# A layer stack on one core: the adaptive-norm weight pieces go to GpSimd's DMA queue, the silu row is made earlier, and their row sums are spread over ten weight slots

## The chip, the core and the metric

One core of a Trainium2 chip runs the whole program as a single launch. The metric is the device time of that launch in microseconds. The core has five instruction streams that run side by side and meet only through semaphores: TensorE (PE, matrix products, with its weight loads shown apart as PEld), VectorE (DVE), ScalarE (ACT), GpSimd (POOL) and SyncE (SP). SP computes nothing here: it waits for semaphores and issues transfers (DMAs). GpSimd can issue transfers too; the trace lists those under a queue of their own.

## What is computed

Two transformer blocks on 256 tokens of width 1024, batch one, in float32. The first has a pooling mixer, a SwiGLU feed-forward, an attention layer with shared keys and values, and a second SwiGLU. The second block is conditioned on a vector `c`: a row of 6 x 1024 modulation values scales, shifts and gates its norms and branches.

```python
def swiglu(h, w_gate_up, w_down):
    gu = h @ w_gate_up
    gate, up = jnp.split(gu, 2, axis=-1)
    return (jax.nn.silu(gate) * up) @ w_down

# first block, two layers:
#   x = x + pool_mixer(rmsnorm(x));  x = x + swiglu(rmsnorm(x))
#   x = x + attention(rmsnorm(x));   x = x + swiglu(rmsnorm(x))

def hybrid_layer(x, c, ada_w, ada_b, ...):
    mod = (jax.nn.silu(c) @ ada_w + ada_b)
    sh1, sc1, g1, sh2, sc2, g2 = jnp.split(mod, 6, axis=-1)
    h = rms_norm(x, norm1_g) * (1 + sc1) + sh1
    ...                      # sparse attention, RWKV branch, mixture of experts
```

The change concerns `mod` alone: how its 24 MB of weights (`ada_w`, 1024 x 6144) come in and when they are multiplied. The two SwiGLU layers (d_ff = 2816) are where that work is hidden.

## The kernel before

**The feed-forward loops.** Each SwiGLU is 22 chunks (`FFN_CHUNKS`) of 128 hidden columns. A chunk's gate, up and down weights are one slot of 1.5 MB; eleven slots (`RING`) form a ring in on-chip memory. A feed-forward is a hardware loop of two turns ("bodies") over eleven slots each. There are two feed-forwards, so four bodies, which the text numbers 1 to 4. Products are made in three passes (high by high, low by high, high by low part), so one slot is 48 matmuls of gate and up and 24 of down, each 128x128 by 256 columns: L724, L725, L726. PE runs gate/up of slot s and then down of slot s-1. In the last step of a body there is only a down product left, since the loop turns there.

**VectorE in a slot** (`ffn`, L1766 to L1788): it makes the low part of the next slot's gate/up weights (L1736, 2048 columns), waits for PE's gate/up result, forms the activation (L1778 to L1784), and makes the low part of this slot's down weights (L1736, 1024 columns). PE needs that second low part for its down product. Three places in this order can take a row sum of the modulation: place 0 ahead of the activation, place 1 between activation and down part, place 2 behind the down part.

**The modulation** (`modulation`, L1764). `ada` holds 96 pieces of 128 x 512 values (256 KB each): each piece is 512 of the 1024 inputs for 128 outputs, and one instruction multiplies it with the matching half of silu(c) and adds its row sum into a column of `mod`. 24 pieces (`ADA_PARTS`) belong to a body. There are two buffers, `ada_part[0]` and `[1]`, so piece p may be loaded when the sum of piece p-2 is done (semaphore `ada_used`). `c_part` is half of silu(c), copied to all 128 partitions; it is reloaded once a body. Before, slots 3 to 10 of a body take three pieces each, slots 0 to 2 none (`ADA_FIRST = 3`).

**silu(c)** lies across the partitions (`csil`, 128 x 8). To be spread over all partitions it is written to a row in main memory, `c_row`, value by value (L532), and read back from there. ACT makes sigmoid(c) at L1408, after the norm that precedes feed-forward 1; DVE multiplies at L1891; SP writes the row at L532 and waits for it at L534.

**What SP does, in its program's order:** the first eleven weight slots; the wait for silu(c), the row and the wait for the row; then, slot after slot, the loads of modulation pieces (`ada_before`, each behind a wait on `ada_used`), and the next load of the ring, which waits until PE has used that place (`w_used`, L542). So one stream, and one hardware queue, carries weight slots and pieces.

**GpSimd before** has nothing to do until it loads the attention bias (`load_toeplitz`, L494) behind feed-forward 1, and its arithmetic (L636) begins behind feed-forward 2.

Of the kernel before, what the change touches and what calls it, by code (L numbers as in the profile page):

```python
# [17 lines left out]
P = 128  # L18
# [26 lines left out]
RING = 11  # L45
# [97 lines left out]
def build(nc, xT, vec, consts, selector, inv_count, pool_w, ws, ada, rel, lora, router, router_bias, experts, final_row, out):  # L143
# [5 lines left out]
    with ExitStack() as ctx:  # L149
# [299 lines left out]
        ADA_FIRST = 3  # L449
# [48 lines left out]
        def _(sp):  # L498
# [18 lines left out]
            def ada_before(s, load_c, load_part, part_used):  # L517

                if s == 1:
                    part_used(-1)  # L520
                    load_c()
                    load_part(0)
                    load_part(1)
                elif s >= ADA_FIRST - 1 and s < RING - 1:
                    for p in range(3 * (s - ADA_FIRST + 1) + 1, 3 * (s - ADA_FIRST + 1) + 4):
                        if 2 <= p < ADA_PARTS:
                            part_used(p - 2)
                            load_part(p)

            sp.wait_ge(csil_ready, 1)  # L530
            with nc.allow_non_contiguous_dma(reason="one column a chunk"):
                sp.dma_start(c_row.rearrange("a (c p) -> p (a c)", p=P), csil).then_inc(csil_ready, 16)  # L532
            sp.wait_ge(csil_ready, 17)
            with sp.Fori(1, S_FFN2 // RING) as i:  # L534
                for s in range(RING):

                    ada_before(s,
                               lambda: sp.dma_start(c_part, c_row[0:1, bass.ds(ADA_COLS * i - ADA_COLS, ADA_COLS)].partition_broadcast(P)).then_inc(ada_landed[0], 16),
                               lambda p: sp.dma_start(ada_part[p % 2], ada[ADA_PARTS * i + (p - ADA_PARTS)]).then_inc(ada_landed[p % 2], 16),
                               lambda p: sp.wait_ge(ada_used, ADA_PARTS * i + (p + 2 - ADA_PARTS)))  # L540
                    sp.wait_ge(w_used, RING * i + (s + 1 - RING))
                    sp.dma_start(slot(s), ws[RING * i + s]).then_inc(landed[s], 16)  # L542
# [13 lines left out]
            def ffn_2_ada(units):  # L556
                for unit in units:
                    body, s = divmod(unit, RING)
                    ada_before(s,
                               lambda: sp.dma_start(c_part, c_row[0:1, body * ADA_COLS:(body + 1) * ADA_COLS].partition_broadcast(P)).then_inc(ada_landed[0], 16),  # L560
# [1875 lines left out]
```

## Time and profile before

| what | value |
|---|---|
| median of 3 runs | 1431.26 us (1429.6 to 1434.93) |
| the profiled execution, its own time | 1436.26 us |
| its span, first to last instruction | 1434.6 us |
| PE busy, DVE busy, ACT busy, POOL busy | 1321.5, 751.1, 510.2, 198.0 us |
| bodies 1 and 2 (feed-forward 1) | from 42.84 to 257.5 us |
| bodies 3 and 4 (feed-forward 2) | from 396.73 to 601.1 us |

The profiled execution took 5.0 us more than the median. The page gives, for each engine, busy time and share; PE's busy time includes stretches in which its matmuls are slow, so the pace is read from the start of one slot to the start of the next. "PEclk" is the granted TensorE clock: 1.00 is 2.4 GHz, 0.50 is 1.2 GHz.

### The profile page before, as it was taken

The numbers are of one execution on the slowest core, as the hardware profiler recorded it, in microseconds if no ns is written. First come the engines' busy times: TensorE is split into PE (matmuls) and PEld (weight loads), VectorE is DVE, ScalarE is ACT, GpSimd is POOL, SyncE is SP. The second block draws the span as 40 slices with busy tenths as digits, with TensorE's granted clock in tenths as the row PEclk, the third lists the DMA queues.
The fourth block names the chain that finished last, engine by engine and source line by source line (L and its number), as shares of the span: only waits on it lengthen the run. The fifth ranks groups of instructions, "written<-read, shape, count | busy, mean of one in ns | idle before, by whom it ended". The sixth has DMA issues, their size and how long they took to land.

```text
span 1434.6 us, 24642 instructions
## 1 busy us (share of the span) xinstructions
PE 1321.5 (92%) x10257; PEld 1017.1 (71%) x10260; DVE 751.1 (52%) x1297; ACT 510.2 (36%) x828; POOL 198.0 (14%) x96
## 2 busy tenths in 40 slices
PE   4989899799999799979998689999999999999997
PEld 3989899789899799878997579754444444444432
DVE  5767687657588768778994645511221212212113
ACT  2423333356543233347553542322222222222212
POOL 0000000000000000076866265100000000000002
PEclk7999999899999999989999999999999999999999
DMA  9776567243377806632422413619999999999994
GB/s 355 274 284 238 209 249 273 78 105 131 148 280 265 301 16 226 223 145 45 176 89 98 169 55 142 255 65 421 427 427 423 426 423 428 423 425 428 423 425 168
DMA packets 50640, 364.40 MB, mean 254 GB/s; under 512 B 7411, under 2 KB 8563, under 8 KB 23924
## 3 DMA queue, kind: packets, MB, share of 16 engines
q1 hardware_dynamic: 49828, 360.61, 63.3%
q0 software_dynamic: 720, 2.46, 0.9%
q8 instruction: 71, 1.16, 0.3%
q14 instruction: 21, 0.17, 0.0%
HBM read 360.35 MB, written 2.70 MB: 253 GB/s over the span
## 4 chain that ended last, share of the span: by engine, by line
PE 67%; DMA 12%; DVE 11%; issue 4%; ACT 3%; POOL 2%; SPq 0%; DVEq 0%; POOLq 0%
PE banks L1266 15%; DMA scr<-ada 9%; PE banks L724 9%; PE banks L726 8%; PE banks L725 8%; PE banks L1291 8%; PE banks L1217 4%; PE banks L1226 4%; DMA c_row<-small 2%; POOL slot_lo L636 2%; PE banks L702 1%; DVE scr L1764 1%; DVE slot_lo L1736 1%; PE banks L713 1%; PE banks L1232 1%
## 5 line engine op out<-in xcount | busy, mean ns | idle before, releaser
L726 PE MATMUL banks<-h_hi,slot_lo 128*128 128x256 f32 x704 | 200.3, 285 | 4.2 <-issue 4.2
L724 PE MATMUL banks<-h_hi,gu_hi 128*128 128x256 f32 x704 | 200.7, 285 | 3.2 <-issue 3.2
L725 PE MATMUL banks<-h_lo,gu_hi 128*128 128x256 f32 x704 | 200.2, 284 | 0.0
L2294 DVE TENSOR_TENSOR out_lo<-banks,out_hi 128x512 fp32r<-128x512 f32 x62 | 42.9, 692 | 185.2 <-ACT out_hi L1678 185.2
L726 PEld LDWEIGHTS banks<-h_hi,slot_lo 128*128 128x128 f32 x704 | 136.2, 193 | 4.5 <-issue 4.5
L724 PEld LDWEIGHTS banks<-h_hi,gu_hi 128*128 128x128 f32 x704 | 136.2, 193 | 4.0 <-issue 3.4
L726 PE MATMUL banks<-slot_lo,slot_lo 128*128 128x256 f32 x480 | 137.0, 285 | 0.0
L725 PEld LDWEIGHTS banks<-h_lo,gu_hi 128*128 128x128 f32 x704 | 136.2, 194 | 0.0
L724 PE MATMUL banks<-act_hi,down_hi 128*128 128x256 f32 x352 | 103.4, 294 | 20.6 <-DVE slot_lo L1736 20.6
L1291 PE MATMUL banks<-ring,scr 128*64 128x512 f32 x512 | 116.9, 598 | 1.9 <-ACT scr L1672 1.9
L1266 PE MATMUL banks<-ring,scr 128*64 128x512 f32 x512 | 112.6, 592 | 0.0
L1266 PE MATMUL banks<-ring 128*64 128x512 f32 x512 | 112.6, 592 | 0.0
L1369 ACT ACTIVATE scr<-scr 128x256 f32<-128x256 f32 x44 | 18.4, 419 | 264.6 <-DVE scr L1778 264.6
L2272 DVE TENSOR_TENSOR scr<-banks,scr 128x256 f32<-128x256 f32 x32 | 13.6, 425 | 184.1 <-ACT scr L1665 184.1
L725 PE MATMUL banks<-act_lo,down_hi 128*128 128x256 f32 x352 | 102.5, 291 | 0.0
L726 PE MATMUL banks<-act_hi,slot_lo 128*128 128x256 f32 x352 | 102.3, 291 | 0.0
L1736 DVE TENSOR_TENSOR slot_lo<-ring,gu_hi 128x2048 fp32r<-128x2048 f32 x44 | 100.6, 2290 | 2.0 <-ACT gu_hi L1357 2.0
L636 POOL TENSOR_TENSOR slot_lo<-ring,win_hi 128x1024 fp32r<-128x1024 f32 x20 | 48.6, 2434 | 327.3 <-ACT win_hi L1485 327.3
L726 PEld LDWEIGHTS banks<-slot_lo,slot_lo 128*128 128x128 f32 x480 | 93.0, 194 | 0.0
L1764 DVE CUSTOM_DVE_ANT_0 scr<-scr,mod 128x512 f32<-128x512 f32 x96 | 71.8, 748 | 34.6 <-DMA scr<-ada 34.6
L1266 PEld LDWEIGHTS banks<-ring,scr 128*64 128x64 f32 x512 | 36.7, 137 | 73.3 <-issue 73.3
L1266 PEld LDWEIGHTS banks<-ring 128*64 128x64 f32 x512 | 36.8, 137 | 73.0 <-issue 73.0
(418 smaller groups left out, 3001.1 us busy)
## 6 DMA issues: line engine op xcount, KB each, us to landing
ring<-experts SPq DMA_DIRECT2D x64, 2048.0 KB, 11.4
ring<-ws SPq DMA_DIRECT2D x77, 1536.0 KB, 7.1
ring<-experts SPq DMA_DIRECT2D x64, 1024.0 KB, 11.0
scr<-ada SPq DMA_DIRECT2D x96, 256.0 KB, 4.0
ring<-experts SPq DMA_DIRECT2D x1, 3072.0 KB, 9.9
scr<-bias_line POOLq DMA_DIRECT2D x4, 512.0 KB, 8.3
bias_line<-scr SPq DMA_DIRECT2D x1, 1536.0 KB
x<-xT SPq DMA_DIRECT2D x1, 1024.0 KB, 4.9
```

Of the source, the lines that this page charges most:

```text
L636: nc.gpsimd.tensor_tensor(dst, src, hi.bitcast(F32), ALU.subtract).then_inc(win_w_lo, 1)
L724: nc.tensor.matmul(out, hi, move_hi, start=start, stop=False, skip_group_check=True)
L725: nc.tensor.matmul(out, hi, move_lo, start=False, stop=False, skip_group_check=True)
L726: return nc.tensor.matmul(out, lo, move_hi, start=False, stop=stop, skip_group_check=True)
L1217: mm = nc.tensor.matmul(bank, tok[:, tb, step * P:(step + 1) * P], pick[buf][:, tb, :], start=(n == 0 and tb == 0), stop=(n == 1 and tb == ...
L1226: mm = nc.tensor.matmul(B[2 * tb + half], spread[k % 2][:, tb * P:(tb + 1) * P], part[:, half * 512:(half + 1) * 512], start=False, stop=F ...
L1266: mm = nc.tensor.matmul(B[4][CAP * j:CAP * (j + 1), :], gathered_h[o][:, c, at:at + CAP], unit(u)[:, c * 512:(c + 1) * 512], start=(c == 0 ...
L1291: mm = nc.tensor.matmul(B[6 + half][CAP * j:CAP * (j + 1), :], act_pt[:, f, CAP * j:CAP * (j + 1)], unit(u)[:, lo:lo + 512], start=(f == 0 ...
L1369: nc.scalar.activation(sig_f[:, s % 2, :], gated[:, s % 2, :], ACT.Sigmoid).then_inc(sig_ready, 1)
L1736: nc.vector.tensor_tensor(slot_lo[PLACE[base + s]][:, lo:to], slot(base + s)[:, lo:to], hi.bitcast(F32), ALU.subtract).then_inc(signal, 1)
L1764: nc.vector.tensor_tensor_reduce(of, of, c_part, 1.0, col, ALU.mult, ALU.add, col).then_inc(ada_used, 1)
L2294: ins = nc.vector.tensor_tensor(out_lo[part], B[6 + half], out_hi[part].bitcast(F32), ALU.subtract)
```

## The change

Four things are changed.

1. The row `c_row`, the copies to `c_part` and all 96 pieces are issued by GpSimd (`load_ada`), two bodies ahead of `load_toeplitz` and two behind it. SP keeps the weight slots alone. GpSimd waits for `gu_ready` once in each feed-forward (the memory of the buffers is in other use before), and for `ada_used` per piece as SP did.
2. sigmoid(c) on ACT and silu(c) on DVE are made beside the pooling mixer, ahead of the norm of feed-forward 1.
3. The 24 row sums of a body sit in slots 1 to 10: places 1 and 2 of slot 1, then two sums (places 0 and 1) in even slots and three in odd ones.
4. The counts that DVE waits for are adapted, since `c_row` and `c_part` now count on other semaphores.

```diff
-        ADA_FIRST = 3
+        ADA_STEPS = [(1, 1), (1, 2), *((s, n) for s in range(2, RING) for n in range(2 + s % 2))]
...
-            sp.wait_ge(csil_ready, 1)
-            with nc.allow_non_contiguous_dma(reason="one column a chunk"):
-                sp.dma_start(c_row.rearrange("a (c p) -> p (a c)", p=P), csil).then_inc(csil_ready, 16)
-            sp.wait_ge(csil_ready, 17)
             with sp.Fori(1, S_FFN2 // RING) as i:
                 for s in range(RING):
-                    ada_before(s, ...
                     sp.wait_ge(w_used, RING * i + (s + 1 - RING))
                     sp.dma_start(slot(s), ws[RING * i + s]).then_inc(landed[s], 16)
...
+            def load_ada(body):
+
+                outputs, half = divmod(body, 2)
+                if half == 0:
+                    pool.wait_ge(gu_ready, FFN_CHUNKS * outputs + 1)
+                pool.wait_ge(ada_used, ADA_PARTS * body + 1)
+                pool.dma_start(c_part, c_row[0:1, half * ADA_COLS:(half + 1) * ADA_COLS].partition_broadcast(P)).then_inc(ada_landed[0], 16)
+                for p in range(ADA_PARTS):
+                    if p >= 2:
+                        pool.wait_ge(ada_used, ADA_PARTS * body + p)
+                    pool.dma_start(ada_part[p % 2], ada[ADA_PARTS * body + p]).then_inc(ada_landed[p % 2], 16)
+
+            pool.wait_ge(csil_ready, 1)
+            with nc.allow_non_contiguous_dma(reason="one column a chunk"):
+                pool.dma_start(c_row.rearrange("a (c p) -> p (a c)", p=P), csil).then_inc(ada_landed[1], 16)
+            pool.wait_ge(ada_landed[1], 16)
+            load_ada(0)
+            load_ada(1)
...
             load_toeplitz(pool, bias1, 0, HEADS_1, bias_loaded)
+            load_ada(2)
+            load_ada(3)
...
             norm_squares(0)
+            act.wait_ge(vec_loaded, 16)
+            nc.scalar.activation(csig, vecs[:, VEC["c"][0]:VEC["c"][1]], ACT.Sigmoid).then_inc(csig_ready, 1)
...
             norm_squares(1, "norm_ffn0")
-            act.wait_ge(vec_loaded, 16)
-            nc.scalar.activation(csig, vecs[:, VEC["c"][0]:VEC["c"][1]], ACT.Sigmoid).then_inc(csig_ready, 1)
             ffn(S_FFN1, 0)
...
-                    p, half = 3 * (s - ADA_FIRST) + n, base // S_FFN2
-                    if p < 0:
+                    if (s, n) not in ADA_STEPS:
                         return
+                    p, half = ADA_STEPS.index((s, n)), base // S_FFN2
...
+            dve.wait_ge(csig_ready, 1)
+            nc.vector.tensor_tensor(csil, csig, vecs[:, VEC["c"][0]:VEC["c"][1]], ALU.mult).then_inc(csil_ready, 1)
+
+            ffn(S_FFN1, 0, 1, "norm_ffn0", first_start, meanwhile=lambda: value_parts(0))
```

SP in feed-forward 1, before: the row, then the loop with pieces between the slots (`ring<-ws` is a weight slot, `scr<-ada` a piece, `weights_used` is `w_used`).

```order
L532 DMA c_row<-small 128x8x1 [waits csil_ready]
L534 UNCONDITIONAL_BRANCH [waits csil_ready]
L534 ISA
L542 ISA [waits weights_used]
L542 DMA ring<-ws 128x3072
L540 ISA
L538 ISA [waits ada_weights_used]
L538 DMA scr<-c_row 128x512
L539 ISA
L539 DMA scr<-ada 128x512
```

The same place now: SP goes from the eleventh slot straight into the loop.

```order
L507 DMA ring<-ws 128x3072 x9
L517 UNCONDITIONAL_BRANCH
L517 ISA
L521 ISA [waits weights_used]
L521 DMA ring<-ws 128x3072
```

GpSimd from its start, now (before, its first transfer is `bias_line`):

```order
L609 DMA c_row<-small 128x8x1 [waits csil_ready]
L601 DMA scr<-c_row 128x512 [waits ada_weights_used,gu_ready,ada_landed1]
L605 DMA scr<-ada 128x512 x2
L605 DMA scr<-ada 128x512 [waits ada_weights_used] x22
L601 DMA scr<-c_row 128x512 [waits ada_weights_used]
L605 DMA scr<-ada 128x512 x2
L605 DMA scr<-ada 128x512 [waits ada_weights_used] x22
L494 DMA scr<-bias_line 32x16x256 [waits proj_ready,line_stored]
```

The row and two bodies' pieces stand ahead of the bias loads; the first `c_part` waits for the row and for the first gate/up result.

DVE at the end of slot 1 of a body, before: activation, down part, next gate/up part, and no row sum.

```order
L1784 TENSOR_TENSOR act_lo_58<-scr,act_hi_56 128x256 [waits dve_step]
L1736 TENSOR_TENSOR slot_lo_60<-ring,down_hi_54 128x1024 [waits down_hi_ready]
L1739 REGISTER_ALU
L1736 TENSOR_TENSOR slot_lo_62<-ring,gu_hi_52 128x2048 [waits gu_hi_ready]
L1778 TENSOR_TENSOR scr<-banks,rinv 128x256 [waits gu_ready]
```

The same place now, up to the first sum of slot 2:

```order
L1770 TENSOR_TENSOR act_lo_58<-scr,act_hi_56 128x256 [waits dve_step]
L1746 ISA
L1749 ISA [waits ada_weights_used]
L1750 ISA scr,mod<-scr,mod 128x512 [waits ada_landed0]
L1750 ISA mod 128x1
L1723 TENSOR_TENSOR slot_lo_60<-ring,down_hi_54 128x1024 [waits down_hi_ready]
L1749 ISA
L1750 ISA scr,mod<-scr,mod 128x512 [waits ada_landed1]
L1750 ISA mod 128x1
L1726 REGISTER_ALU
L1723 TENSOR_TENSOR slot_lo_62<-ring,gu_hi_52 128x2048 [waits gu_hi_ready]
```

The first sum, with its wait for piece 0 and `c_part`, now stands ahead of slot 1's down part; before, the first one stood two slots later.

## Rows read from the trace of the kernel before

**Rows 1.** The page: PE's busy time, and the chain's shares by line.
```profile
PE 1321.5 (92%) x10257; PEld 1017.1 (71%) x10260; DVE 751.1 (52%) x1297; ACT 510.2 (36%) x828; POOL 198.0 (14%) x96
PE banks L1266 15%; DMA scr<-ada 9%; PE banks L724 9%; PE banks L726 8%; PE banks L725 8%; PE banks L1291 8%; PE banks L1217 4%; PE banks L1226 4%; DMA c_row<-small 2%; POOL slot_lo L636 2%; PE banks L702 1%; DVE scr L1764 1%; DVE slot_lo L1736 1%; PE banks L713 1%; PE banks L1232 1%
```

**Rows 2.** Windows, one a body (start:end, length, busy times, clock, DMA share, GB/s).
```profile
core 0: us, PE busy (x) PEld busy (x) DVE busy (x) ACT busy (x) POOL busy (x), PEclk, DMA share, GB/s
42.84:156.09 113.25, 100.37 (x795) 99.48 (x793) 82.64 (x139) 38.30 (x38) 0.00 (x0) 0.94 0.70 257
156.09:257.50 101.41, 97.37 (x794) 97.20 (x792) 76.91 (x136) 34.59 (x34) 0.00 (x0) 0.97 0.65 235
396.73:497.40 100.67, 95.52 (x792) 95.17 (x793) 83.48 (x140) 37.83 (x36) 0.00 (x0) 1.00 0.73 277
497.40:601.10 103.70, 97.81 (x791) 97.34 (x792) 75.74 (x141) 32.79 (x33) 0.00 (x0) 0.95 0.42 146
```

**Rows 3.** DVE's waits for pieces, bodies 1 to 4 (total us, times, longest).
```profile
DVE scr L1764 <- DMA scr<-ada: 23.3, 9, 11.1
...
DVE scr L1764 <- DMA scr<-ada: 7.6, 8, 2.3
...
DVE scr L1764 <- DMA scr<-ada: 2.9, 5, 0.9
...
DVE scr L1764 <- DMA scr<-ada: 0.8, 1, 0.8
```

**Rows 4.** Windows over PE's gaps; columns as in rows 2.
```profile
80.33:85.60 5.27, 0.28 (x3) 0.10 (x2) 4.94 (x12) 3.17 (x3) 0.00 (x0) 0.83 0.65 262
145.30:151.30 6.00, 0.27 (x3) 0.08 (x2) 3.67 (x9) 4.75 (x4) 0.00 (x0) 0.78 1.02 419
248.10:252.40 4.30, 0.30 (x3) 0.10 (x1) 2.05 (x5) 2.58 (x3) 0.00 (x0) 0.84 0.97 346
488.90:491.10 2.20, 0.25 (x3) 0.07 (x2) 2.04 (x4) 2.20 (x2) 0.00 (x0) 1.00 0.61 139
493.90:503.60 9.70, 2.36 (x11) 1.89 (x9) 2.14 (x1) 0.00 (x0) 0.00 (x0) 0.65 0.77 271
596.30:598.30 2.00, 0.30 (x4) 0.13 (x2) 2.00 (x5) 0.78 (x2) 0.00 (x0) 1.00 0.45 86
```

**Rows 5.** Timeline of DVE, one steady slot of body 3 (start, duration, what).
```profile
434.48 0.43 DVE L1778 TENSOR_TENSOR scr<-banks,rinv 128x256 f32<-128x256 f32 x1 [0.70 <-PE banks L726]
...
436.98 0.74 DVE L1764 CUSTOM_DVE_ANT_0 scr<-scr,mod 128x512 f32<-128x512 f32 x1
...
438.79 0.75 DVE L1764 CUSTOM_DVE_ANT_0 scr<-scr,mod 128x512 f32<-128x512 f32 x1
...
441.66 0.75 DVE L1764 CUSTOM_DVE_ANT_0 scr<-scr,mod 128x512 f32<-128x512 f32 x1
...
443.12 0.42 DVE L1778 TENSOR_TENSOR scr<-banks,rinv 128x256 f32<-128x256 f32 x1 [0.70 <-PE banks L726]
```

**Rows 6.** The chain in order of time, and the DMA load meanwhile (columns: rows 2).
```profile
44.86 25.38 DMA c_row<-small
71.78 8.60 DMA scr<-ada
86.32 6.27 DMA scr<-ada
...
42.84:51.48 8.64, 8.64 (x73) 8.62 (x72) 6.46 (x10) 5.44 (x8) 0.00 (x0) 1.00 1.00 421
```

**Rows 7.** DMA: issues with us to landing; GpSimd's queue from 902 to 914 us.
```profile
scr<-ada SPq DMA_DIRECT2D x96, 256.0 KB, 4.0
scr<-router POOLq DMA_DIRECT2D x1, 256.0 KB, 7.1
dense_rows<-ring POOLq DMA_DIRECT2D x1, 64.0 KB, 1.9
...
q0 software_dynamic: 112, 0.30, 15.8%
```

**Rows 8.** Timeline of ACT ahead of feed-forward 1.
```profile
38.15 0.51 ACT L1341 ACTIVATE h_hi<-x,vecs 128x256 fp32r<-128x256 f32 x1 [2.35 <-DVE x L1861]
```

More of the change, by code:

```diff
@@ L516, in _ @@
                 load(n)
[L517 to L528, printed above, removed]
-            sp.wait_ge(csil_ready, 1)
-            with nc.allow_non_contiguous_dma(reason="one column a chunk"):
-                sp.dma_start(c_row.rearrange("a (c p) -> p (a c)", p=P), csil).then_inc(csil_ready, 16)
-            sp.wait_ge(csil_ready, 17)
             with sp.Fori(1, S_FFN2 // RING) as i:
                 for s in range(RING):
[L537 to L540, printed above, removed]
                     sp.wait_ge(w_used, RING * i + (s + 1 - RING))
@@ L554, in _ @@
             load_after(S_FFN2 + 6, s_ready, HEADS_1 // 2)
[L556 to L560, printed above, removed]
-                               lambda p: sp.dma_start(ada_part[p % 2], ada[ADA_PARTS * (2 + body) + p]).then_inc(ada_landed[p % 2], 16),
-                               lambda p: sp.wait_ge(ada_used, ADA_PARTS * (2 + body) + p + 2))
-            ada_units = 0
             for n in range(S_FFN2 + 7, N_SLOTS):
@@ L573, in _ @@
                         sp.dma_start(gate_row.rearrange("a (c p) -> p (a c)", p=P), mod[:, 40:48]).then_inc(rows_loaded, 16)
-                after = TENANT[n] + 1 if n >= S_FFN2 + RING else S_FFN2
-                if n < S_BR and after > S_FFN2 + ada_units:
-                    ffn_2_ada(range(ada_units, min(after - S_FFN2, FFN_CHUNKS)))
-                    ada_units = after - S_FFN2
-                load_after(n, w_used, after)
+                load_after(n, w_used, TENANT[n] + 1 if n >= S_FFN2 + RING else S_FFN2)
             def load_gate_up(u, e):
@@ L1760, in modulation @@
                     of, col = ada_part[p % 2], mod[:, half * ADA_PARTS + p:half * ADA_PARTS + p + 1]
-                    c_loads = 1 - p % 2
-                    a_body = 8 * ADA_PARTS + 16 * c_loads
-                    dve.wait_ge(ada_landed[p % 2], a_body * i + (2 * a_body * half + 16 * (p // 2 + 1 + c_loads)))
+                    a_body = 8 * ADA_PARTS + (0 if p % 2 else 16)
+                    dve.wait_ge(ada_landed[p % 2], a_body * i + (2 * a_body * half + 16 * (p // 2 + 2)))
                     nc.vector.tensor_tensor_reduce(of, of, c_part, 1.0, col, ALU.mult, ALU.add, col).then_inc(ada_used, 1)
@@ L1887, in first_start @@
                 h_lo_pair(3)
-            def silu_of_c():
-                dve.wait_ge(csig_ready, 1)
-                nc.vector.tensor_tensor(csil, csig, vecs[:, VEC["c"][0]:VEC["c"][1]], ALU.mult).then_inc(csil_ready, 1)
-            ffn(S_FFN1, 0, 1, "norm_ffn0", first_start, silu_of_c, meanwhile=lambda: value_parts(0))
+            dve.wait_ge(csig_ready, 1)
+            nc.vector.tensor_tensor(csil, csig, vecs[:, VEC["c"][0]:VEC["c"][1]], ALU.mult).then_inc(csil_ready, 1)
+            ffn(S_FFN1, 0, 1, "norm_ffn0", first_start, meanwhile=lambda: value_parts(0))
             dve.wait_ge(rt_ready, 3)
```

## The prediction

> **What bounds the kernel now.** I read the page's chain first. The last chain runs mostly through PE's matmuls, but 9% of the span is `DMA scr<-ada`, 2% `DMA c_row<-small` and 1% the row sums [rows 1]. PE is busy 92% by its own row, yet that row does not tell where it is slow, so I went to windows, one a body. All four bodies hold the same 792 matmuls, and they take 113.25, 101.41, 100.67 and 103.70 us [rows 2]. The pace inside is one slot in 443.12 - 434.48 = 8.64 us [rows 5], or 0.12 us a matmul; eleven slots are 95.0 us. The rest is idle time of PE or a slow clock. The third view, DVE's waits, shows who sits ahead of PE: DVE waited for pieces of `ada` for 23.3, 7.6, 2.9 and 0.8 us in bodies 1 to 4 [rows 3]. So PE sets the pace in a steady slot (DVE idles 0.70 us there, waiting for PE [rows 5]), and the pieces set it at a few places of feed-forward 1.
>
> **A clean body.** At a body's end PE has no gate/up product to run while DVE makes activation and down part. In bodies 3 and 4 that gap is 2.20 and 2.00 us at clock 1.00 [rows 4]. A clean body is thus 95.0 + 2.2 = 97.2 us. Body 3 confirms it: its last 3.5 us (493.9 to 497.4) are a further gap at the loop's turn [rows 4], and 100.67 - 3.5 = 97.2. Body 4 begins with a gap of that kind again and some slow matmuls (9.70 us with 2.36 busy over the turn [rows 4]); neither is a wait for DVE.
>
> **What goes.** Body 1 is 113.25 - 97.2 = 16.0 us above clean, body 2 101.41 - 97.2 = 4.2 us. Their parts stand in rows 4: a gap of 5.27 us where the first row sum waited, one of 6.00 at the end of body 1 and one of 4.30 at the end of body 2, where 2.1 would be normal; in each the clock is under 1.00, and the matmuls after it run at half of it for some microseconds. Body 1's first wait comes from the row: the chain has `c_row` from 44.86 for 25.38 us, then the first pieces for 8.60 us [rows 6]; the DMA engines are at share 1.00 with the ring's first eleven slots when it is issued [rows 6], so it lay behind them. The later waits come from a piece issued right behind a weight slot in SP's queue, 6.27 us [rows 6] where the median piece lands in 4.0 [rows 7]. If all of these go, 20.2 us are won. That is an upper end, by rows of two undisturbed bodies.
>
> **The row and silu.** DVE ends the mixer at about 30.7 us, and csil (0.2 us) fits ahead of its next wait. ACT gets two more changes of its function table; it later waits 2.35 us for DVE's x [rows 8], and the norm's last squares come behind that wait, so I cost them at nothing (at most one such wait, 2.4 us, if they fell behind it). GpSimd can issue the row at 31 us. `c_part` may not go before the first gate/up result, 42.84 + 48 x 0.12 = 48.6 us, so the row has 17 us. Its bounds: 1.9 us (GpSimd's small store on idle engines [rows 7]) and 39 us (landing at 70 as before, that is, only when the ring's loads are through). I take some 10 to 15 us, hidden. The reason: in the window of the router loads GpSimd's queue shows 112 packets for two transfers of 128 rows each, completions included [rows 7]; so it joins rows to packets, and 1024 values of 4 bytes should be few packets that need not each wait for one of the ring's.
>
> `c_part` and piece 0, issued at 48.6 us with the ring's loads still running: 7.1 us for the first by the router's load, which also ran beside a weight stream [rows 7], and some 2.5 for the second behind it, 58.2 us. DVE could use them at 42.84 + 96 x 0.12 + 2.5 = 56.9 us; PE needs slot 1's down part at 42.84 + 168 x 0.12 = 63.0 us, and sum and down part take 1.9 us ([rows 5], from 436.98 to the next sum's 438.79, and a little), so 61.1 is early enough. Cost nothing, 3 us of cover.
>
> **The pieces.** 24 sums remain 24 sums; ten slots instead of eight carry them, 2.4 a slot. In a steady slot with three sums DVE still idles 0.70 us [rows 5], so no slot becomes DVE's. The question is the landing time L of a piece from GpSimd. The tightest buffer is the one freed by place 1 of an odd slot and used by place 0 of the next: from 436.98 + 0.75 = 437.73 to 441.66 is 3.93 us [rows 5]. Just then (24 matmuls, 2.9 us, after the gate/up result) SP issues a weight slot. DVE's activation is late only by x = L - 3.93 - 0.70 = L - 4.6. In mid-body PE does not see x below 1.4 us (its next gate/up product lasts 48 x 0.12 = 5.76 us, and DVE's down part is ready at 438.79 + 0.1 - 434.48 = 4.4), at a body's end it sees all of it. Bounds for L: 1.9 us and 7.1 us [rows 7]. I take 5.5, nearer the upper one, since a slot is in flight, though not the endless stream of the router's row. x = 0.9: nothing in mid-body, 4 x 0.9 = 3.6 us at four ends.
>
> **Where the pieces were, and what is late next.** SP no longer waits for the row or for `ada_used`; its slots go out when PE frees them. Behind GpSimd's waits only its bias loads are queued (295 us before, due behind feed-forward 1, when bodies 1 and 2 are through) and its arithmetic behind feed-forward 2. With the pieces on time the next bound is PE. Nothing else moves; all later stages begin earlier by the gain.
>
> **Sum.** 20.2 - 3.6 = 16.6 us. On the profiled span: 1434.6 - 16.6 = 1418.0. That execution lay 5.0 above the median (1436.26 to 1431.26); on the median 1431.3 - 16.6 = 1414.7.
>
> **Rivals.**
>
> *A. The row is late all the same.* If 1024 tiny writes alternate one for one with the ring's packets, they end with the ring's loads and the row lands at 70. Then piece 0 lands at some 75, DVE's down part of slot 1 is ready at 76.9, and PE idles from 63.0 to 76.9 with a slow clock behind (2.5 us): 16.4 us given back, 1431. For it: nothing shows a scattered write on GpSimd's queue. Against: the packets of rows 7.
>
> *B. GpSimd's own queue does not help a piece.* It lands as late beside a slot as from SP, 6.3 us [rows 6]. x = 1.7: 4 x 1.7 at the ends and 0.3 in 16 pairs of slots, 11.6 us; gain 8.6, 1422.7. The Trainium skill says just this (DMA: Bandwidth & Descriptors, "Issuing engines are not separate DMA queues"): engines' transfers share the same DMA engines, and issuing from several saves only issue time. Against: SP's piece stands behind the slot in one stream, GpSimd's beside it, and rows 7 have a load of the same size landing in 7.1 us only beside the longest stream.
>
> *C. Slower.* L is 7.1 us whenever a slot is in flight. x = 2.5: 10 us at four ends and 1.1 us in each of 16 mid-body pairs, 17.6; together 27.6 against 20.2, 1438.7. It decides from 20x - 22 = 20.2, x = 2.1, L = 6.7 us. For it: the router's row. Against: that row has a stream of experts without a pause, here DMA share is 0.42 to 0.73 [rows 2].
>
> *D. A gap at the loop's turn in feed-forward 1.* At 493.9 to 503.6 PE stands some 8 us and is slow for 2 more, waiting for nothing the profile names [rows 4]. Body 1 to 2 shows none, but PE came out of a 6.00 us gap at a slow clock there. If it appears with the gap shortened, 10 us go: 1424.7. Against: PE's program is unchanged.
>
> **Chances and range.** Forecast 0.56, A 0.13, B 0.12, C 0.10, D 0.08. A measurement of this kernel can tell 0.5%, 7.2 us. Under 1424.1 lie the forecast, most of B and some of D: 0.68; within 0.5% A and the rest: 0.21; slower C and what I have not thought of: 0.11. Range: the low end has L under 4.6, 1411, and allows 4 us for a shorter gap at the turn of feed-forward 2, now that less runs in SP's queue; the high end reaches A. 1407 to 1431.5, which leaves C out.
>
> **What the profile after would show.** Windows of the four bodies: 98, 98, 101.5 and 104.5 us. No gap near the start of body 1; `c_row` landed before 48 us; DVE's waits for pieces under 10 us in sum, at place 0 of even slots. Ends of bodies: 3 us gaps at clock 1.00. A is seen as one wait of 14 us at the first sum, B and C as equal small waits in every pair of slots, D as a gap behind body 1's last down product. The forecast is wrong if GpSimd's landings pass 6.7 us or the row passes 52 us.

## The result: slower by 1.2%

| kernel | median (us) | lowest to highest | runs | span and time of the profiled run |
|---|---|---|---|---|
| before | 1431.24 | 1429.60 to 1434.93 | 4 | 1434.6, 1436.26 |
| after | 1444.98 | 1442.88 to 1454.64 | 4 | 1441.2, 1443.04 |

The ratio of the medians is 1.0117, interval 1.0086 to 1.0148. The forecast was 1414.7, with a range of 1407 to 1431.5, so its sign was wrong. The profiled spans differ by 6.6 us and the medians by 13.7. The profiled run of before lies 5 us above its median and that of after 2 below, so what follows sets spans against spans, and only the size of the result is taken from the medians.

The page of the kernel after answers to [rows 1]. PE is as busy as before (1322.0 us against 1321.5), but pieces of `ada` now take 13% of the chain, where it was 9%. In the costliest groups (busy us, mean ns of one, then idle before it and its releaser) the row sum has 65.3 us of waiting for pieces, over the whole run:

```profile
PE 1322.0 (92%) x10260; PEld 1018.0 (71%) x10260; DVE 749.6 (52%) x1297; ACT 512.6 (36%) x830; POOL 252.5 (18%) x197
PE banks L1253 15%; DMA scr<-ada 13%; PE banks L1278 8%; PE banks L711 7%; PE banks L713 7%; PE banks L712 7%; PE banks L1204 4%; PE banks L1213 4%; DVE scr L1750 2%; DVE slot_lo L1723 2%; POOL slot_lo L623 2%; PE banks L689 1%; PE banks L700 1%; PE banks L1219 1%; DMA c_row<-small 1%
L1750 DVE CUSTOM_DVE_ANT_0 scr<-scr,mod 128x512 f32<-128x512 f32 x96 | 71.7, 748 | 65.5 <-DMA scr<-ada 65.3
scr<-ada POOLq DMA_DIRECT2D x96, 256.0 KB, 4.9
```

The windows of the four bodies answer to [rows 2], with the same columns (length, busy times, clock, DMA share, GB/s):

```profile
41.77:154.54 112.77, 98.38 (x795) 97.42 (x793) 82.76 (x138) 38.16 (x37) 15.13 (x28) 0.95 0.76 285
154.54:256.97 102.43, 96.89 (x793) 96.51 (x792) 76.10 (x135) 34.56 (x34) 11.83 (x22) 0.98 0.62 225
397.06:502.07 105.01, 97.12 (x792) 96.57 (x793) 83.18 (x140) 37.79 (x36) 15.07 (x28) 0.98 0.73 269
502.07:609.22 107.15, 99.77 (x791) 99.30 (x792) 75.34 (x141) 32.77 (x33) 11.84 (x22) 0.94 0.42 141
```

They sum to 427.4 us, against 419.0 in [rows 2]. So the four bodies are 8.3 longer, and the rest of the span is 1.7 shorter. The forecast had 402 in sum, so the miss is 25.4 us in these four windows. That is all of it: the whole span missed by 23.2 (forecast 1418.0, measured 1441.2).

DVE's waits for pieces, bodies 1 to 4, against [rows 3] (total us, times, longest), show the same: where bodies 3 and 4 had 2.9 and 0.8 us of them, they now have 15.4 and 10.4.

```profile
DVE scr L1750 <- DMA scr<-ada: 24.2, 12, 3.4
...
DVE scr L1750 <- DMA scr<-ada: 15.3, 8, 3.4
...
DVE scr L1750 <- DMA scr<-ada: 15.4, 9, 2.6
...
DVE scr L1750 <- DMA scr<-ada: 10.4, 3, 5.4
```

Windows over the four gaps at the ends of bodies answer to [rows 4]. In a clean body this gap is 2 us; here it is 8.6, 4.5, 4.7 and 4.4:

```profile
141.00:149.60 8.60, 0.32 (x3) 0.12 (x1) 4.95 (x14) 4.96 (x4) 1.49 (x3) 0.66 0.57 213
248.20:252.70 4.50, 0.34 (x4) 0.16 (x2) 4.25 (x11) 4.11 (x4) 0.00 (x0) 1.00 0.67 227
491.00:495.70 4.70, 0.29 (x3) 0.09 (x2) 4.45 (x12) 4.05 (x4) 0.96 (x2) 0.97 0.77 261
600.70:605.10 4.40, 0.26 (x3) 0.06 (x2) 4.11 (x11) 2.85 (x4) 0.00 (x0) 0.94 0.70 243
```

**The row did what was forecast.** The chain in order of time (start, duration, what) has its landing 12.56 us behind its issue, and then one late piece after another, in each group of the same buffer:

```profile
30.43 12.56 DMA c_row<-small
...
49.00 9.91 DMA scr<-ada
59.99 7.85 DMA scr<-ada
68.92 7.33 DMA scr<-ada
77.32 7.08 DMA scr<-ada
...
124.52 7.90 DMA scr<-ada
133.50 6.75 DMA scr<-ada
141.33 6.24 DMA scr<-ada
```

**How long a piece takes.** The issues around the largest gap, from the timelines of SP and GpSimd (start, duration, what, idle before it and its releaser), with the three sums of DVE that waited. SP's row covers three slots; they were in flight from 124.2 to 132.2, 132.9 to 140.1 and 141.5 to 148.5:

```profile
124.22 17.61 SPq L521 DMA_DIRECT2D ring<-ws  x3
...
124.52 0.54 POOL L605 DMA_DIRECT2D scr<-ada  x1 [4.13 <-DVE mod L1750]
133.50 0.54 POOL L605 DMA_DIRECT2D scr<-ada  x1 [5.28 <-DVE mod L1750]
141.33 0.54 POOL L605 DMA_DIRECT2D scr<-ada  x1 [4.11 <-DVE mod L1750]
...
132.45 0.75 DVE L1750 CUSTOM_DVE_ANT_0 scr<-scr,mod 128x512 f32<-128x512 f32 x1 [1.72 <-DMA scr<-ada]
140.27 0.75 DVE L1750 CUSTOM_DVE_ANT_0 scr<-scr,mod 128x512 f32<-128x512 f32 x1 [2.76 <-DMA scr<-ada]
147.59 0.75 DVE L1750 CUSTOM_DVE_ANT_0 scr<-scr,mod 128x512 f32<-128x512 f32 x1 [3.39 <-DMA scr<-ada]
```

SP issued a slot at 124.22, GpSimd the piece 0.3 us later, and it landed at 132.42, with the slot (7.90 us). Another piece, issued at 114.88 some 0.7 us ahead of a slot, landed in 2.90. DVE used the late piece late, so the buffer came free late and the next piece fell beside the next slot too: 7.90, 6.75, 6.24. The waits grow (1.72, 2.76, 3.39), and the body's end shows them. Where no slot is in flight, as in body 4 from 523 to 536 us, the same loads land in 2.9:

```profile
scr<-ada POOLq DMA_DIRECT2D x4, 256.0 KB, 2.9
```

The landing time follows the distance between the two issues. The table has the 80 pieces of after that went out later than 90 us and are not the first two of a body, and the 84 of before by the same rule. It gives the us to landing (lowest, median, highest) and the number of pieces:

| the piece is issued | GpSimd's queue, after | SP's queue, before |
|---|---|---|
| with no slot in flight, the next more than 0.5 us off | 2.8, 2.9, 5.0 (18) | 2.5, 2.6, 3.0 (23) |
| 0.35 to 0.5 us ahead of a slot | 3.3, 3.3, 3.3 (2) | 2.5, 2.6, 3.1 (11) |
| less than 0.35 us ahead of a slot | 4.6, 6.2, 8.2 (11) | none |
| up to 1.2 us behind a slot | 6.2, 6.7, 7.9 (8) | 6.1 (1) |
| 1.2 to 2 us behind | 5.8, 5.8, 5.9 (3) | 5.7, 6.1, 7.5 (23) |
| 2 to 3 us behind | 4.8, 5.2, 6.7 (15) | 5.0, 5.2, 5.5 (2) |
| 3 to 4 us behind | 4.0, 4.7, 5.6 (12) | 3.6, 4.2, 4.8 (4) |
| 4 to 5 us behind | 3.6, 3.7, 4.2 (4) | 3.5, 3.9, 5.3 (20) |
| more than 5 us behind | 2.8, 3.0, 4.2 (7) | none |

At the same distance behind a slot the two queues differ little. What differs is the place ahead of it. SP's program sets the order, and its piece is 0.35 us or more ahead; GpSimd's piece goes out when its buffer is freed, and if it is less than 0.35 us ahead it is late already.

### The profile page after: what moved, and what is told of

The parts are those of the page before. It is cut to its first block, busy times and chain, and to the rows that moved or that the text cites. A ratio compares the mean times of both kernels' runs of the same rounds, so it can differ in the third digit from the quotient of the medians.

```text
span 1441.2 us, 24502 instructions
## 1 busy us (share of the span) xinstructions
PE 1322.0 (92%) x10260; PEld 1018.0 (71%) x10260; DVE 749.6 (52%) x1297; ACT 512.6 (36%) x830; POOL 252.5 (18%) x197
## 3 DMA queue, kind: packets, MB, share of 16 engines
q8 instruction: 71, 1.16, 0.3%
## 4 chain that ended last, share of the span: by engine, by line
PE 62%; DMA 15%; DVE 13%; issue 4%; ACT 3%; POOL 2%; DVEq 0%; SPq 0%; POOLq 0%
PE banks L1253 15%; DMA scr<-ada 13%; PE banks L1278 8%; PE banks L711 7%; PE banks L713 7%; PE banks L712 7%; PE banks L1204 4%; PE banks L1213 4%; DVE scr L1750 2%; DVE slot_lo L1723 2%; POOL slot_lo L623 2%; PE banks L689 1%; PE banks L700 1%; PE banks L1219 1%; DMA c_row<-small 1%
## 5 line engine op out<-in xcount | busy, mean ns | idle before, releaser
L605 POOL DMA_DIRECT2D scr<-ada x96 | 51.7, 539 | 322.6 <-DVE mod L1750 318.6
L1750 DVE CUSTOM_DVE_ANT_0 scr<-scr,mod 128x512 f32<-128x512 f32 x96 | 71.7, 748 | 65.5 <-DMA scr<-ada 65.3
L663 POOL TENSOR_TENSOR ring<-ring,x 128x512 f32<-128x512 f32 x4 | 5.0, 1273 | 479.3 <-DVE ring L2270 479.3
L711 PEld LDWEIGHTS banks<-act_hi,down_hi 128*128 128x128 f32 x352 | 70.6, 201 | 25.4 <-issue 25.4
```

The costliest lines, as they stand in the source:

```text
L605: pool.dma_start(ada_part[p % 2], ada[ADA_PARTS * body + p]).then_inc(ada_landed[p % 2], 16)
L711: nc.tensor.matmul(out, hi, move_hi, start=start, stop=False, skip_group_check=True)
L1750: nc.vector.tensor_tensor_reduce(of, of, c_part, 1.0, col, ALU.mult, ALU.add, col).then_inc(ada_used, 1)
```

## The experiments

Two theories went in. One: the queue is at fault, since a piece on GpSimd's queue shares the engines with a slot issued at the same moment, where SP's program could put it ahead. The other: the new places are at fault, with a tight buffer in each second slot. Each ratio is to before, timed beside it (medians 1429.3 to 1430.2); only that of after, 1.0117, is the one of the result. Experiments 5, 6, 8 and 9 also write SP's loop out instead of turning it.

### 1. The row alone

Before, with silu beside the mixer and the row from GpSimd; pieces on SP in their old places.

```diff
-            sp.dma_start(c_row.rearrange("a (c p) -> p (a c)", p=P), csil).then_inc(csil_ready, 16)
-            sp.wait_ge(csil_ready, 17)
+            sp.wait_ge(row_stored, 16)
...
+            pool.wait_ge(csil_ready, 1)
+            pool.dma_start(c_row.rearrange("a (c p) -> p (a c)", p=P), csil).then_inc(row_stored, 16)
```

> Before, with one part of the change alone: silu(c) made beside the mixer and the row written from GpSimd's queue. Pieces stay in SP's queue in the old order and the old slots 3 to 10. Theory 1 (the row was late, and the loss of the change comes from the pieces' queue): the first gap of body 1 (5.3 us and its slow clock, about 8 us in all) goes, bodies 2 to 4 stay; about 1423 us. Rival (the scattered write slows the ring's loads so much that its early place costs): no gain or a loss, 1431 or more.

Measured: 1424.13 (1421.68 to 1429.90, 10 runs), ratio 0.9958, interval 0.9933 to 0.9983. About 1423 was expected. This part of the change is worth 6 us by itself. Body 1 takes 106.65 instead of 113.25, and its 5.3 us gap is gone. At its end a gap of 5.87 stays.

### 2. The queue alone

After, with the old places.

```diff
-        ADA_STEPS = [(1, 1), (1, 2), *((s, n) for s in range(2, RING) for n in range(2 + s % 2))]
+        ADA_STEPS = [(s, n) for s in range(3, RING) for n in range(3)]
```

> The changed kernel with the old placing: three sums in slots 3 to 10, all pieces from GpSimd. Theory 1 (a piece issued beside a weight slot lands in about 7 us from GpSimd): the piece freed by place 1 and used by place 0 of the next slot is now late in every slot, 2.5 us each, of which 1.1 reach PE in mid-body: some 30 us above before, 1450 to 1465. Rival (the new placing is to blame, the queue is harmless): 1415 to 1425.

Measured: 1461.42 (1453.40 to 1468.09, 4 runs), ratio 1.0193, interval 1.0154 to 1.0233. That lies in the 1450 to 1465 expected. The bodies are 113.28, 111.34, 114.21 and 111.74, with PE gaps of 0.9 to 3.1 us inside them: five, six, four and one. Against the first experiment, which has the same places and the same early row, only the pieces' queue differs: 0.0235 of the time, 34 us. The page has 80.4 us of waits for pieces, where that of the first experiment has 30.2:

```profile
L1750 DVE CUSTOM_DVE_ANT_0 scr<-scr,mod 128x512 f32<-128x512 f32 x96 | 71.8, 748 | 80.4 <-DMA scr<-ada 80.4
```

They are not only at the buffer that the expectation named: 20.5 us of them are there (freed by place 1, used by place 0 of the next slot), 41.8 at pieces freed by place 0 and used by place 2 of the same slot, and 18.2 at pieces freed by place 2 and used by place 1 of the next. So the time came out as expected, and the mechanism only in part.

### 3. The places alone

The first experiment with the new places. The pieces stay on SP. A piece whose buffer is freed by place 1 goes ahead of the slot, one freed by place 2 behind it. `c_part` and piece 0 go out right behind the first gate/up result.

```diff
+        def ada_issue(p):
+            s, n = ADA_STEPS[p - 2]
+            return s if n == 2 else s - 1
...
+                for p in range(2, ADA_PARTS):
+                    if ada_issue(p) == s:
+                        part_used(p - 2)
+                        load_part(p)
```

> The changed kernel with the pieces back in SP's queue, in SP's old rule (the piece freed by place 1 goes out ahead of the weight slot, the one freed by place 2 behind it); silu and row early, sums spread over ten slots. Theory 1: the loss goes, 1412 to 1420. Rival (the new placing is to blame): like the changed kernel, 1435 to 1447.

Measured: 1429.88 (1424.74 to 1434.64, 10 runs), ratio 0.9988, interval 0.9962 to 1.0014: no difference from before, and not the 1412 to 1420 expected. One wait stands against the gain. Once past it, bodies 1 and 2 hold nothing but end gaps of 2 us (body 2 is 96.89), and so do bodies 3 and 4 but for the loop's turn. The wait is a new one: `c_part`, issued at 48.54, landed at 68.72, and PE stood from 62.22 to 73.93. A window over 60 to 70 us has only 2.5 us of PE in it:

```profile
60.00:70.00 10.00, 2.50 (x21) 2.30 (x20) 0.00 (x0) 0.00 (x0) 0.00 (x0) 0.78 0.79 325
```

DVE's timeline has the wait that ends it, in brackets:

```profile
71.89 0.75 DVE L1771 CUSTOM_DVE_ANT_0 scr<-scr,mod 128x512 f32<-128x512 f32 x1 [15.14 <-DMA scr<-ada]
```

On SP's queue `c_part` and the first pieces lie behind what is left of the eleven slots that SP issued at the start. In after's trace the first piece, issued at 49.00 on GpSimd's queue, landed in 9.91. So a queue of its own does help against a backlog, and harms against a slot that SP could have held back.

### 4. Both pieces of a slot ahead of it

The first experiment, old places; a piece freed by place 2 goes ahead of the slot too.

```diff
+        ADA_STEPS = [(s, n) for s in range(3, RING) for n in range(3)]
...
+            return s - 1
```

> As e1 (row and silu early, pieces from SP, sums in slots 3 to 10), but SP issues the pieces freed by places 1 and 2 of a slot both ahead of the weight slot, not only the first of them. Theory 1: no piece that is needed soon lies beside a weight slot, all gaps but the 2 us at a body's end go: about 1412. Rival (DVE's own work or the ring bounds the slots): as e1.

Measured: 1427.72 (1423.34 to 1433.91, 10 runs), ratio 0.9977, interval 0.9956 to 0.9998, not the 1412 or so that I expected. The median landing fell to 2.9 us, but a slot now waits for DVE's last sum. Bodies 108.43, 99.63, 102.49 and 104.49: end gaps of 3.3 us in bodies 1 and 3 and of 2.0 in 2 and 4, and a gap of 3.79 at the turn of feed-forward 1. That gap is a wait for a piece too. The last sum of the body waited for it, and the next body's first gate/up low parts stand behind that sum:

```profile
145.30 0.75 DVE L1768 CUSTOM_DVE_ANT_0 scr<-scr,mod 128x512 f32<-128x512 f32 x1 [2.96 <-DMA scr<-ada]
145.98 4.49 DVE L1740 TENSOR_TENSOR slot_lo<-ring,gu_hi 128x2048 fp32r<-128x2048 f32 x2
150.60 0.55 PE L728 MATMUL banks<-h_hi,gu_hi 128*128 128x256 f32 x1 [3.52 <-DVE slot_lo L1740]
```

The median hides why nothing is won: the waits changed place. In the first experiment DVE waits 30.2 us for pieces, 20.3 of them for pieces freed by place 2. Here those are down to 1.0, but the slot, held back, now goes out some 2.3 us ahead of the piece freed by place 0 of the next slot. Such a piece lands in 5.1 by the median, at most 7.9, it is wanted at place 2 of the same slot, and the waits for it are 28.5 us of 38.6.

### 5. A slot held until the piece has landed

After, with one wait more in SP's program: a slot goes out when the piece that place 1 frees is there.

```diff
+                    p = ADA_STEPS.index((s + 1, 1)) + 2
+                    each = 192 if p % 2 else 208
+                    sp.wait_ge(ada_landed[p % 2], each * k + (16 * (p // 2 + 2) - each * back))
```

> The changed kernel, pieces still from GpSimd and sums in the new places; only SP is changed: it holds each next weight slot until the piece freed by place 1 has landed, so that this piece never lies beside a slot. Theory (a piece beside a weight slot takes 7 us, alone 2.9; that is the whole price of the queue): the gaps at the ends of bodies fall from 4.4 to 8.6 us to about 2, median near e3's, 1428 to 1434. Rival (GpSimd's own path is slow or starved by VectorE, whatever else is in flight): as the changed kernel, 1440 to 1450.

Measured: 1453.63 (1452.45 to 1455.63, 4 runs), ratio 1.0151, interval 1.0098 to 1.0205. Expected were 1428 to 1434. The rival's 1440 to 1450 was missed too, and its mechanism is not seen: in body 2 the held pieces land in 2.8 to 4.0, by the median 2.9, and over the run the waits at the buffer of place 1 to place 0 fall from 33.3 us in after to 5.9. The slot then goes out 0.02 us after the held piece has arrived, and the pieces behind it lie beside that slot: one issued at 134.30 beside a slot of 133.3 took 6.40, one issued at 141.78 beside a slot of 141.3 took 7.58. Bodies 1 to 3 end with gaps of 8.68, 8.35 and 8.14, and DVE waits 71.6 us for pieces in all. Holding back a slot for one chain of pieces hands the collision to the other, and the order has to be right for both.

### 6. Fewer slots ahead, pieces on SP

The third experiment, with six slots issued at the start instead of eleven and SP six ahead from there on. It takes away the backlog that the third one ran into.

```diff
-            for n in range(RING):
+            AHEAD = 6
+            for n in range(AHEAD):
...
+                n = chunk + AHEAD
+                if n >= RING:
+                    sp.wait_ge(w_used, n + 1 - RING)
+                load(n)
```

> e3 (sums spread, pieces in SP's queue, row and silu early) with the ring's first loads cut from eleven slots to six before the first c_part; SP's loop is written out and stays six slots ahead. Theory (e3's only loss is an 11.7 us gap in body 1, where c_part and the first pieces lie behind 9 MB of ring loads that nobody needs yet): that gap goes, with its slow clock some 14 us, 1414 to 1419. Rival (six slots ahead are too few, PE waits for weights): new gaps on landed slots, 1430 or more.

Measured: 1414.79 (1411.40 to 1417.84, 4 runs), ratio 0.9890, interval 0.9836 to 0.9943, inside the 1414 to 1419 expected. Windows of the four bodies:

```profile
42.39:139.53 97.14, 95.44 (x795) 95.24 (x794) 81.30 (x138) 38.19 (x36) 0.00 (x0) 1.00 0.69 257
139.53:236.50 96.97, 95.27 (x794) 95.04 (x792) 77.69 (x136) 34.58 (x34) 0.00 (x0) 1.00 0.65 246
372.34:472.98 100.64, 95.51 (x792) 95.16 (x793) 83.46 (x140) 37.81 (x36) 0.00 (x0) 1.00 0.74 277
472.98:576.60 103.62, 98.01 (x792) 97.49 (x792) 75.61 (x141) 32.78 (x33) 0.00 (x0) 0.95 0.43 146
```

Bodies 1 and 2 are clean at full clock. DVE waits 6.2 us for pieces in all four bodies, at most 1.3 at a time:

```profile
DVE scr L1776 <- DMA scr<-ada: 6.2, 8, 1.3
```

The issues of `ada` over the whole run land in 2.4 us at best, which is ahead of a slot, and 9.0 at worst:

```profile
DMA to landing us min/median/max: 2.4/3.6/9.0
```

### 7. The order on SP alone

Before with nothing changed but the order of the fourth experiment.

```diff
+        def ada_issue(p):
+            s, n = ADA_STEPS[p - 2]
+            return s - 1
```

> The kernel before with SP's order alone changed: the piece freed by place 2 goes out ahead of the weight slot. Row and silu late as before. Theory (the row's wait of 25 us is one loss, pieces behind a slot another): body 1's first gap stays, its end gap of 6.0 us shrinks to about 2 to 3; 1423 to 1429. Rival (holding the slot back costs as much as the piece wins): 1430 or more.

Measured: 1433.25 (1425.97 to 1439.26, 10 runs), ratio 1.0006, interval 0.9979 to 1.0033. Expected were 1423 to 1429. As in the fourth experiment nothing comes of it: in the profiled run the end gap of body 1 shrinks from 6.0 to 3.2, and over ten runs no gain is left. The waits moved here as well: those for pieces freed by place 2 fall from 19.9 us to none, those for pieces freed by place 0 rise from none to 24.8.

### 8. Without GpSimd

The sixth experiment with the row from SP, so that GpSimd's queue carries nothing of this.

```diff
-                pool.dma_start(c_row.rearrange("a (c p) -> p (a c)", p=P), csil).then_inc(row_stored, 16)
+                sp.dma_start(c_row.rearrange("a (c p) -> p (a c)", p=P), csil).then_inc(row_stored, 16)
```

> e8 with the row written by SP again, behind six weight slots, as soon as silu(c) is ready (31 us); GpSimd takes no part. Theory (the row need not pass the ring on a queue of its own, it must only be early and have little ahead of it): lands before 60 us, time as e8, 1411 to 1418. Rival (only GpSimd's packing of the 1024 values makes the row quick): row at 65 us or later, a gap in body 1, 1422 or more.

Measured: 1414.42 (1412.19 to 1422.69, 5 runs), ratio 0.9917, interval 0.9887 to 0.9947. The row went out at 30.9 us and took 18.8, where GpSimd's took 14.1 in the sixth experiment, and landed at 49.7. `c_part` followed and landed in 4.9, still in time. The two versions can't be told apart, so GpSimd's queue isn't needed for the row either.

### 9. Fewer slots ahead, pieces on GpSimd

After, with SP six slots ahead.

```diff
-            with sp.Fori(1, S_FFN2 // RING) as i:
-                for s in range(RING):
-                    sp.wait_ge(w_used, RING * i + (s + 1 - RING))
-                    sp.dma_start(slot(s), ws[RING * i + s]).then_inc(landed[s], 16)
+            for n in range(AHEAD, S_FFN2):
+                sp.wait_ge(w_used, min(n - AHEAD + 1, FFN_CHUNKS))
+                load(n)
```

> The changed kernel (pieces from GpSimd, sums spread) with SP loading six slots before the loop and then staying six ahead. Theory (the ring's backlog is a small part of the changed kernel's loss, the pieces beside slots are the large one): the gaps in the first half of body 1 go, those at the bodies' ends stay, 1436 to 1444. Rival (the backlog is the large part): 1425 or less.

Measured: 1441.70 (1439.16 to 1452.40, 4 runs), ratio 1.0111, interval 1.0061 to 1.0161, inside the 1436 to 1444 that the queue theory gave. The four bodies take 106.55, 105.99, 106.14 and 107.04, with end gaps of 9.81, 4.34, 4.79 and 4.14. The sums wait for pieces as in after:

```profile
DVE scr L1749 <- DMA scr<-ada: 64.2, 29, 5.1
```

Against the sixth experiment, with its places and its early row, the ratio differs by 0.022, 32 us; against the eighth, timed beside this one, by 0.019, 28 us. (Here SP's loop is also kept to a fixed lead, so the moments at which slots go out are not quite the same.)

### What the runs say together

| pieces on | old places | new places | new places, six ahead |
|---|---|---|---|
| SP | 0.9958 | 0.9988 | 0.9890 |
| GpSimd | 1.0193 | 1.0117 | 1.0111 |

Row and silu are early in all six. The queue costs in each column: 34, 18 and 32 us. The middle one is smaller because the SP version pays the 11.7 us wait for `c_part` there and some slow clock behind it. The theory of the places falls: on GpSimd's queue the new ones save 11 us, and on SP's they bring clean bodies once the backlog is gone. Old places with six slots ahead were not run, so of the 10 us between the first and the sixth experiment the shares of the places and of the shorter lead are not known one by one.

## Why the prediction was wrong, by its steps

- **What bounds the kernel, and the clean body: right.** The price of 97.2 us is confirmed by the sixth experiment at 97.1 and 97.0, and so is the "upper end" of 20.2 us: its bodies 1 and 2 are 20.6 shorter than those of [rows 2]. That its median is the forecast figure is no merit of the forecast, which spoke of another kernel.
- **The row: right.** It was put at 10 to 15 us and took 12.56. The reason given, few packets, is borne out: GpSimd's queue has it as 16 packets of 256 bytes, while the window of SP's row in before has 1112 packets under 512 bytes, completions included. Silu cost nothing that shows. Rival A did not come in this form.
- **`c_part` and piece 0: right in time**, 58.91 against 58.2. But DVE's first sum ran late all the same: the next pieces of that buffer took 7.1 to 7.9 us beside what remained of the ring's first slots, which were late themselves (below). So PE had gaps of 2.44, 2.90, 1.36 and 0.50 us between 70.6 and 106.5, 7.2 us that no step held.
- **The cost of a late piece, x = L - 4.6 with one L of 5.5: the step that failed.** It took one landing time for all pieces, looked at one buffer (freed by place 1 of an odd slot, used by place 0 of the next) and started each pair with DVE on time. It had x = 0.9, nothing in mid-body and 3.6 us at four ends; measured were 13.8 at ends, 3.5 in mid-body and DVE late nearly throughout.
  - *The size of L.* Where DVE had been on time until then, the piece went out 0.6 to 1.1 us behind a slot, and in the four such cases of bodies 2 to 4 it landed in 6.2 to 6.9, not in 5.5. Over all 20 pieces of this kind landings run from 2.9 to 7.9 us with a median of 5.3. So 5.5 was near the middle, and the middle was the wrong thing to take: a late DVE issues the next piece later behind the slot, where it lands faster, and stays late all the same. In bodies 1 and 2 the activation began 1.7 to 6.3 us after PE's result in every slot from 2 on.
  - *The other buffers.* Of the 65.3 us that DVE waits for pieces, 33.3 are at this kind. The other 32 are at kinds that had no term: 14.8 from place 0 to place 2 of the same slot (by [rows 5] its cover, the time between freeing and use, is 447.43 - 442.41 = 5.0 us, not much more than 3.9), 8.8 from place 0 to place 0 of the next slot, 5.2 from place 2 to place 1, and 3.3 at the first two pieces of a body.
  - *The ends.* 2.1 + (L - 4.6) turned round gives 6.9, 7.2 and 7.0 for the gaps of 4.44, 4.71 and 4.45 of bodies 2 to 4. Only in body 4 is that the landing time. In bodies 2 and 3 the piece landed in 4.9, and there the formula fits by luck: DVE had begun the activation of the slot before already 2.0 and 2.3 us late. In body 4 it had begun on time. The last late piece of bodies 2, 3 and 4, its issue and the sum that waited:

```profile
242.54 0.54 POOL L605 DMA_DIRECT2D scr<-ada  x1 [2.63 <-DVE mod L1750]
247.44 0.75 DVE L1750 CUSTOM_DVE_ANT_0 scr<-scr,mod 128x512 f32<-128x512 f32 x1 [3.40 <-DMA scr<-ada]
...
485.61 0.54 POOL L605 DMA_DIRECT2D scr<-ada  x1 [2.63 <-DVE mod L1750]
490.52 0.75 DVE L1750 CUSTOM_DVE_ANT_0 scr<-scr,mod 128x512 f32<-128x512 f32 x1 [1.74 <-DMA scr<-ada]
...
593.02 0.54 POOL L605 DMA_DIRECT2D scr<-ada  x1 [4.09 <-DVE mod L1750]
599.92 0.75 DVE L1750 CUSTOM_DVE_ANT_0 scr<-scr,mod 128x512 f32<-128x512 f32 x1 [5.38 <-DMA scr<-ada]
```

- **What mid-body hides: a second error, in the other direction.** The prediction had PE miss DVE's down part from x = 1.4 us on, with one gate/up product (5.76 us) in between. There is the down product of the slot before as well. In before's steady slot PE turns to it at 434.27, to the next gate/up at 437.15 and to this slot's down product at 442.92, while DVE has the down part by 438.9. The cover is 4.0 us, not 1.4. It cost the forecast nothing, whose x was 0.9, but it put 4.8 and 17.6 us too much into rivals B and C. Without them C would have said 1421.1. What PE did see in mid-body came by another way: a late sum at place 2 holds back the next gate/up low part, which stands behind it. Two rows of before's PE have its turn to the next gate/up and to the down product; two of after have the sum that waited and PE behind it:

```profile
437.15 0.28 PE L724 MATMUL banks<-h_hi,gu_hi 128*128 128x256 f32 x1
442.92 0.28 PE L724 MATMUL banks<-act_hi,down_hi 128*128 128x256 f32 x1
...
210.65 0.75 DVE L1750 CUSTOM_DVE_ANT_0 scr<-scr,mod 128x512 f32<-128x512 f32 x1 [2.92 <-DMA scr<-ada]
213.67 0.39 PE L711 MATMUL banks<-h_hi,gu_hi 128*128 128x256 f32 x1 [1.38 <-DVE slot_lo L1723]
```

- **Each end for itself.** At the end of body 1 three late pieces in a row added up to a gap of 8.59, 6.5 above clean, since a late piece frees its buffer late. None of the three is of the buffer that was priced. Elsewhere in mid-body PE had only two gaps of over a microsecond, 1.66 and 1.83, both of the kind just shown.
- **Rival C came nearest, in part by luck.** It put L at 7.1 whenever a slot is in flight and gave back 27.6 us. On the profiled spans before and after, 20.2 less and 27.6 more make 1434.6 + 7.4 = 1442.0, and 1441.2 was measured. It had 10 us at ends and 17.6 in 16 pairs of slots; measured were 28.6 (427.4 less 419.0 - 20.2): 13.8 at ends, 3.5 in pairs, 7.2 behind the row, and 4 of slow clock and small change. So its sum is closer than its parts: the landings of the pieces that it priced have a median of 5.3, and its equal costs in 16 pairs are not there. Its 1438.7 on the median was low by 6.3, since I took before's 5 us between profiled run and median for granted. It got a chance of 0.10, against a row of the trace that showed a load of this size on this queue beside a stream, 7.1 us [rows 7]. I set that row aside with an average: a DMA share of 0.42 to 0.73 over a body says nothing of the moment at which a piece goes out, and that moment is tied to a slot.
- **Rival B** had the same cause at 6.3 us. Its words were that GpSimd's queue does not help a piece, and the table of landing times shows it: not behind a slot. The Trainium skill (DMA: Bandwidth & Descriptors, "Issuing engines are not separate DMA queues") says that issuing from several engines saves only the issue time, as the transfers share the DMA engines. Here the trace agrees and goes further: what was lost is the order. SP's program put a piece ahead of a slot, and it landed in 2.5 to 3.1; in after, the piece has to win a race against that slot.
- **Rival D** did not come in the kernel after: at 154.5 us PE has no such gap. That of 3.79 in the fourth experiment is another thing, a wait for DVE.
- **The signs announced** were of use. "The forecast is wrong if GpSimd's landings pass 6.7 us" is what happened. B and C were to be "equal small waits in every pair of slots"; they are unequal, for the reason under mid-body.

## What to carry to other kernels

A small load that is wanted soon and a large one that is wanted late belong on one queue, in the order in which they are wanted; moved to a queue of its own, the small one runs beside whatever goes out at the same moment and lands with it. Price it by its distance from the stream's load, here 2.9 us alone, 6.7 right behind a slot, 3.7 four to five us behind; one mean value or a mean DMA share hides this. Then do so for each buffer that the new order makes, and carry an engine's lateness on from one step to the next instead of starting each on time. When an order is put right at the front of a queue, look at how deep the queue already is: eleven slots issued ahead cost 11.7 us at the first piece, six cost nothing.

## What the runs showed of the hardware

**Scattered writes slowed down the loads beside them.** The row is 4 KB, stored as 1024 single values. In after its packets began between 34.97 and 35.93 us, and it landed at 42.99. From 35 to 43 us the loads of the ring fell from the 429 GB/s of before in the same stretch to 156, with the engines' share at 1.16 (columns as in rows 2; after, then before):

```profile
35.00:43.00 8.00, 6.53 (x33) 4.87 (x32) 6.48 (x14) 5.68 (x11) 0.00 (x0) 1.00 1.16 156
```

```profile
35.00:43.00 8.00, 6.47 (x29) 4.76 (x28) 6.48 (x14) 4.27 (x10) 0.00 (x0) 1.00 1.00 429
```

That is some 2.2 MB of loads not made, 5 us at full rate. The last of the eleven slots landed at 74.1 instead of 65.1, and PE did not need it. In the third experiment, with the same row but no pieces from GpSimd, it landed at 70.6, so some 5.5 us of the delay go to the row and the rest to the pieces. It is the pieces behind that met the longer backlog. The writes show in the trace as 16 packets of 256 bytes on GpSimd's queue, 64 values each. Written from SP as single values, the row took longer and held the loads up less: from 35 to 40 and from 40 to 45 us they ran at 192 and 237 GB/s in the eighth experiment, and at 109 and 52 in the sixth with GpSimd's row. The Trainium skill (DMA: Bandwidth & Descriptors, "SWDGE vs HWDGE vs iDMA") has 64 descriptors as a packet's limit, and says that a DMA engine goes round between its queues; the trace agrees on the 64. Why so few packets hold up the others for 7 us the trace does not show.

**A landing time set by the distance between two issues.** 256 KB landed in 2.8 to 3.0 us alone from GpSimd, with one of 18 at 5.0, and in 2.5 to 3.0 from SP. Up to 1.2 us behind 1.5 MB it took 6.2 to 7.9 from GpSimd, and less the later it went out, down to 3.6 to 4.2 at 4 to 5 us (3.5 to 5.3 from SP). Ahead of the large load it stayed short, 2.5 to 3.1 from SP and 3.3 from GpSimd, but less than 0.35 us ahead it took 4.6 to 8.2 from GpSimd (the table of the result has all of it).

**What stays open.** At the turn of the loop in feed-forward 2 PE stands for 3.7 and 4.2 us even in the sixth experiment, and for no reason that the waits name. The trace has a hint. On the queue for instructions (q8) a load of 16 KB begins inside each of the two gaps, at 470.3 and 476.5 us; body 4 has eight such loads, while body 2, into which PE turns without such a gap, has none. In a window over both gaps:

```profile
q8 instruction: 2, 0.03, 1.0%
```

So PE may have waited for code there. That is argued and not shown: no run here changed PE's program.
